# Loading w_down in two row halves per partition instead of row pairs, and the activation product that goes with it

## The chip, the cores and the metric

One Trainium2 chip, one core of it. The time is that of one execution on the device, in microseconds (us), the median of several runs. Engines: PE (TensorE), DVE (VectorE), ACT (ScalarE), POOL (GpSimd), SP (SyncE, which here only issues transfers), and 16 DMA engines that carry out the transfers.

## What is computed

One inference step of a decoder layer for 256 prompt tokens and 8 decode tokens, all float32: a token mixer (retention and gated delta net), then a mixture of experts, and a final norm. The change touches the experts alone. Each token goes to 4 of 32 experts; model and hidden width are both 1024:

```python
def expert_block(args):
    xb, e = args
    hb = (xb @ w_gate_up[e] + b_gate_up[e]).astype(f32)
    glu = jnp.minimum(hb[:, :D_FF], SWIGLU_LIMIT)
    lin = jnp.clip(hb[:, D_FF:], -SWIGLU_LIMIT, SWIGLU_LIMIT)
    act = (glu * jax.nn.sigmoid(SWIGLU_ALPHA * glu) * (lin + 1.0)).astype(xb.dtype)
    return act @ w_down[e] + b_down[e]
```

`w_gate_up` is 32 x 1024 x 2048, `w_down` 32 x 1024 x 1024, 402 MB together, each read once.

## The kernel before, in words

The mixer takes the first third of the time. It loads w_in, the branch weights and w_out in pieces of 2 MB into two slots (`wslot`), with rows of 512 floats (2 KB); the retention states come in rows of 1 KB.

Then come 32 blocks, one for each expert, of 64 token slots each, and after them extra blocks for experts with more tokens, as many as the routing asks for. In a block, PE gathers its tokens by a one-hot product (L1190), transposes them (L1198), multiplies them by gate_up (L1213) into two PSUM banks, and DVE and ACT make the activation: bias (L2300, L2301), clamps, sigmoid (L1648), and as the last product `ac` = `lin` * `sg` (L2313). In `ac` partition 64g+t holds token t and hidden columns 512g to 512g+511. PE transposes `ac` in four tiles of 128 columns (L1222), ACT copies the result to `acT` (L1653), PE multiplies by down (L1237), ACT copies the result to `yb`, and PE adds it to the tokens with the gate weights (L1261, L1268); DVE sums that into X (L2324).

The weights pass through a ring of 16 slots of 1 MiB, 8 KB in each of 128 partitions. SP issues one DMA per slot, in the order of the list `CHUNKS`, written out by hand: for block b four chunks of gate_up, two of down of block b-1, two of gate_up, two of down, two of gate_up; at the end the 8 down chunks of the last two blocks. Before chunk i SP waits until PE has used chunk i-16 (`m_use`). A gate_up chunk is 128 rows of 2048 floats, one row per partition. A down chunk is 256 rows of 1024 floats, two rows per partition. Its matmuls take the two halves of a slot one after the other, each with one column block of `acT`:

```python
for a in range(2):
    for g in range(2):
        t = pe.matmul(home[64 * g:64 * g + 64, :], block_of(acT, 2 * k + a),
                      w[:, D * a + 512 * g:D * a + 512 * g + 512], ...
```

PE works in one fixed order: combine of block b-2, two gate_up chunks of b, transposes of `ac` of b-1, two gate_up chunks, two down chunks of b-1, two gate_up, two down, the gather for b+1, one gate_up, transposes of the tokens, one gate_up. The first four ring chunks are issued during the branch products, eight more (and the first two of down among the next) while w_out is loaded and multiplied; from chunk 16 on each waits for PE.

For an expert known only at run time (an extra block) the same functions `load_chunk` and `activate` are used. The profiled execution has none: L1213 counts 2048 matmuls, 64 for each of 32 blocks.

Of the kernel before, what the change touches and what calls it, by code (L numbers as in the profile page):

```python
# [14 lines left out]
ALU = mybir.AluOpType  # L15
# [6 lines left out]
P = 128  # L22
# [76 lines left out]
def build_layer(nc, d, o):  # L99

    with ExitStack() as ctx:
        base = [-(-nc.sbuf_base // 32) * 32]

        def at(name, offset, shape, dt=F32):
            return nc.alloc_sbuf_tensor_at(name, shape, dt, offset=offset)
# [10 lines left out]
        def sem(name):  # L116
            return ctx.enter_context(nc.semaphore(name))
# [104 lines left out]
        def mnew(name, shape, dt=F32):  # L222
            n = 4
            for x in shape[1:]:
                n *= x
            t = at(name, mb[0], shape, dt)
            mb[0] += -(-n // 32) * 32
            assert mb[0] <= p0 + PREG, mb[0]
            return t
# [17 lines left out]
        xg, glu, lin, xT = [mnew(n, [P, 512]) for n in ("xg", "glu", "lin", "xT")]  # L247
# [13 lines left out]
        sg, ac, acT, yb = [at(n, k0 + 4 * C_NEG + 2048 * i, [P, 512]) for i, n in enumerate(("sg", "ac", "acT", "yb"))]  # L261
        ring = [at(f"ring{k}", (wreg + 65536 + 8192 * k, wreg + 32768 + 8192 * (k - 4), p0 + 8192 * (k - 8),
                                wreg + 8192 * (k - 12))[k // 4], [P, 2 * D]) for k in range(RING)]
# [20 lines left out]
        def half_rows(f):  # L284
            return f.rearrange("p (a n) -> p a n", a=2)

        def half(f, i):

            return f[:, 4 * i:4 * i + 4, :]
# [95 lines left out]
        m_w = [sem(f"m_w{k}") for k in range(RING)]  # L385
# [7 lines left out]
        def after(eng, s, per, b, plus=0):  # L393


            if isinstance(b, int) and b * per + plus <= 0:
                return
            eng.wait_ge(s, b * per + plus)
# [11 lines left out]
        def used(eng, kind, b):  # L410

            if isinstance(b, int):
                if b >= 0:
                    eng.wait_ge(m_use, PLACE[kind, b, KT - 1 if kind == "gate_up" else 3] + 1)
                return
            after(eng, m_use, 12, b, KT if kind == "gate_up" else 12)
# [25 lines left out]
        def _(sp):  # L442
# [28 lines left out]
            for b in range(KT):  # L471
                rows = slice(NBASE * b, NBASE * b + NBASE)
# [5 lines left out]
            for a in range(4):  # L478
                rows, first = slice(32 * a, 32 * a + NBASE), 32 * (a % 2) + NBASE
# [9 lines left out]
            for b in range(KT):  # L489
                rows, first = slice(NBASE * b, NBASE * b + NBASE), NBASE * (b % 4)  # L490
# [56 lines left out]
            def expert(table, e):  # L547
                if isinstance(e, int):
                    return table[0][e]
                return table[0][bass.ds(e, 1)].rearrange("a n m -> (a n) m")  # L550

            def load_chunk(kind, e, k, slot):
                if kind == "gate_up":
                    sp.dma_start(ring[slot][:, :], expert(d["w_gate_up"], e)[P * k:P * k + P, :]).then_inc(m_w[slot], 16)
                else:
                    sp.dma_start(ring[slot][:, :], expert(d["w_down"], e)[2 * P * k:2 * P * k + 2 * P, :].rearrange(  # L556
                        "(p a) n -> p (a n)", a=2)).then_inc(m_w[slot], 16)

            def load_bias(b, e):
                after(sp, m_bb, 1, b, -1)  # L560
# [3 lines left out]
            def load_next(first, last):  # L564
                for i in range(first, last):
                    kind, b, k = CHUNKS[i]
                    if i >= RING:
                        sp.wait_ge(m_use, i - RING + 1)
                    load_chunk(kind, b, k, i % RING)
# [20 lines left out]
            def extra(j, b):  # L590
                e = sp.value_load(xei[0:1, bass.ds(j, 1)], min_val=0, max_val=NE - 1)
                after(sp, m_use, 12, b)
                for k in range(KT):
                    load_chunk("gate_up", e, k, k)
                load_bias(b, e)
                for k in range(4):
                    load_chunk("down", e, k, KT + k)
# [1201 lines left out]
        def _(dve):  # L1799
            link = chain(dve, dve_chain)  # L1800
            v = nc.vector
# [143 lines left out]
            for c in range(2):  # L1945
                for i in range(2):
                    MM.wait(dve, f"QK{i}.{c}")
                    f = half(DT[:, c], i)
# [28 lines left out]
            for c in range(2):  # L1977
# [3 lines left out]
                for q in range(2):  # L1981
                    rows = slice(64 * q, 64 * q + 32)
# [43 lines left out]
            for n, f, first in (("k", k4, 0), ("v", v4, 2 * P)):  # L2026
                MS.wait(dve, "v")
                for j in range(4):
                    rows = slice(32 * j, 32 * j + NB)
# [10 lines left out]
            for j in range(4):  # L2040
                rows = slice(32 * j, 32 * j + NB)
# [117 lines left out]
            for c in range(2):  # L2159
                RA.wait(dve, f"rr{c}")  # L2160
                link(v.tensor_tensor(by_head(oT[c][:, :, :]), by_head(oT[c][:, :, :]), bc(rr[c][:, :, :], 2, 2), ALU.mult))
                f = gT[:, :, P * c:P * c + P]
                RD.did(v.tensor_tensor(f, f, oT[c][:, :, :], ALU.mult), f"g{c}")
            for s in range(4):
                RP.wait(dve, f"out{s}")
                for h in range(RH):
                    f = Ssr[s][:, :, h, :]
# [7 lines left out]
            f = gT[:, :, 2 * P:TOK]  # L2175
# [117 lines left out]
            def activate(b):  # L2293

                used(dve, "gate_up", b)
                if isinstance(b, int) and b == 0:
                    dve.wait_ge(s_bb, 32)
                after(dve, m_bb, 1, b)
                after(dve, m_act, 1, b)
                v.tensor_tensor(glu[:, :], B[0][:, :], bgb[:, 0, :], ALU.add).then_inc(m_b1, 1)  # L2300
                v.tensor_tensor(lin[:, :], B[1][:, :], bgb[:, 1, :], ALU.add).then_inc(m_b2, 1)  # L2301
                after(dve, m_b1, 1, b, 1)
                v.tensor_scalar(glu[:, :], glu[:, :], 7.0, None, ALU.min).then_inc(m_glu, 1)
                after(dve, m_b2, 1, b, 1)
                v.tensor_scalar(lin[:, :], lin[:, :], 7.0, -7.0, ALU.min, ALU.max).then_inc(m_lin, 1)  # L2305
                after(dve, m_lin, 1, b, 1)
                after(dve, m_glu, 1, b, 1)
                v.scalar_tensor_tensor(lin[:, :], lin[:, :], 1.0, glu[:, :], ALU.add, ALU.mult).then_inc(m_lin2, 1)  # L2308
                after(dve, m_lin2, 1, b, 1)
                after(dve, m_sig, 1, b, 1)  # L2310
                after(dve, m_ta, 1, b)
                rows = [f[:, :].rearrange("p (i n a) -> p i n a", n=P, a=2) for f in (lin, sg)]
                v.tensor_tensor(ac[:, :].rearrange("p (i a n) -> p i n a", n=P, a=2), *rows, ALU.mult).then_inc(m_act, 1)  # L2313

            homes = ((B[6], B[7]), (B[2], B[3]))

# [11 lines left out]

            onehot(1, 1)
            activate(0)  # L2330
            dve.wait_ge(s_xaev, 5)
            for b in range(1, NE):
                accumulate(b - 1)
                if b + 1 < NE:
                    onehot(b + 1, b + 1)
                weighted(b - 1, b - 1, b - 1)
                if b == 2:
                    extras()
                activate(b)
# [5 lines left out]
            def extra(j, b):  # L2345
                q = dve.value_load(xqi[0:1, bass.ds(j, 1)], min_val=NE, max_val=NE * NM - 1)
                e = dve.value_load(xei[0:1, bass.ds(j, 1)], min_val=0, max_val=NE - 1)
                onehot(b, q)
                activate(b)
                weighted(b, q, e)  # L2350
                accumulate(b + 1)
                after(dve, m_acc, 3, b, 6)
                dve.sem_inc(m_end)
# [38 lines left out]
```

## Time and profile before

| | us |
|---|---|
| median of 3 runs | 1442.37 |
| lowest, highest | 1439.89, 1442.53 |
| the profiled execution, its own time | 1442.37 |
| its span, first to last instruction | 1440.5 |

| engine | busy us | share of the span |
|---|---|---|
| PE, matmuls | 1387.7 | 96% |
| DVE | 516.9 | 36% |
| ACT | 255.0 | 18% |
| POOL | 108.5 | 8% |

The profile is of one execution. Busy time is that of the instructions themselves; waits stand apart. The shares are means over the span: which resource sets the end in a stretch is read from that stretch. A packet is one contiguous piece that one DMA engine moves. The core read 468.85 MB from memory and wrote 11.26 MB.

### The profile page before, as it was taken

The numbers are of one execution on the slowest core, as the hardware profiler recorded it, in microseconds if no ns is written. First come the engines' busy times: TensorE is split into PE (matmuls) and PEld (weight loads), VectorE is DVE, ScalarE is ACT, GpSimd is POOL, SyncE is SP. The second block draws the span as 40 slices with busy tenths as digits, with TensorE's granted clock in tenths as the row PEclk, the third lists the DMA queues.
The fourth block names the chain that finished last, engine by engine and source line by source line (L and its number), as shares of the span: only waits on it lengthen the run. The fifth ranks groups of instructions, "written<-read, shape, count | busy, mean of one in ns | idle before, by whom it ended". The sixth has DMA issues, their size and how long they took to land.

```text
span 1440.5 us, 18174 instructions
## 1 busy us (share of the span) xinstructions
PE 1387.7 (96%) x7559; PEld 668.5 (46%) x7559; DVE 516.9 (36%) x1097; ACT 255.0 (18%) x465; POOL 108.5 (8%) x107
## 2 busy tenths in 40 slices
PE   8999999999999999999999999999999999999996
PEld 6888985478887433333333332323223332233331
DVE  5655244314112229224323422243222432224323
ACT  3443341122201311011111101111011110111112
POOL 0002110100000001001000100010000100001000
PEclk9999899999999999999999999999999999999999
DMA  7532437544549799999999999999999999999995
GB/s 232 201 126 84 147 103 235 192 162 167 199 138 391 267 408 421 420 421 420 421 421 420 421 420 421 422 421 420 421 420 421 421 421 421 421 421 421 420 421 209
DMA packets 114930, 481.20 MB, mean 334 GB/s; under 512 B 17599, under 2 KB 38511, under 8 KB 65267
## 3 DMA queue, kind: packets, MB, share of 16 engines
q1 hardware_dynamic: 113796, 478.61, 83.4%
q8 instruction: 61, 1.00, 0.3%
q10 hardware_dynamic: 954, 1.07, 0.3%
q0 software_dynamic: 96, 0.33, 0.1%
q14 instruction: 23, 0.19, 0.0%
HBM read 468.85 MB, written 11.26 MB: 333 GB/s over the span
## 4 chain that ended last, share of the span: by engine, by line
PE 60%; DMA 36%; DVE 2%; SPq 1%; issue 1%; ACT 0%; DVEq 0%; ACTq 0%
DMA ring<-in_w_down 36%; PE bank L1213 13%; PE bank L1237 9%; PE bank L688 7%; PE bank L676 6%; PE bank L1085 4%; PE bank L955 4%; PE bank L1190 3%; PE bank L1108 2%; PE bank L1261 2%; DVE Ssg L2073 1%; PE bank L661 1%; SPq L556 1%; PE bank L1198 1%; PE bank L1222 1%; PE bank L948 1%
## 5 line engine op out<-in xcount | busy, mean ns | idle before, releaser
L1213 PE MATMUL bank<-ring,xT 128*64 128x512 f32 x2048 | 477.9, 601 | 6.9 <-DMA ring<-in_w_gate_up 5.5
L1213 PEld LDWEIGHTS bank<-ring,xT 128*64 128x64 f32 x2048 | 134.5, 137 | 277.6 <-issue 247.3
L1237 PE MATMUL bank<-ring,acT 128*64 128x512 f32 x1024 | 236.3, 596 | 21.5 <-DMA ring<-in_w_down 20.8
L2300 DVE TENSOR_TENSOR glu<-bank,bgb 128x512 f32<-128x512 f32 x32 | 22.1, 691 | 598.9 <-PE bank L1213 598.9
L1237 PEld LDWEIGHTS bank<-ring,acT 128*64 128x64 f32 x1024 | 69.8, 137 | 178.9 <-issue 123.1
L688 PE MATMUL bank<-HT,wslot 128*128 128x264 f32 x512 | 119.3, 388 | 0.0
L1787 POOL PARTITION_BROADCAST bgb<-bgu x31 | 40.8, 1316 | 998.4 <-DVE lin L2301 781.4
L688 PEld LDWEIGHTS bank<-HT,wslot 128*128 128x128 f32 x512 | 95.3, 190 | 19.6 <-issue 4.6
L1663 ACT COPY yb<-bank 128x512 f32<-128x512 f32 x32 | 18.7, 586 | 438.0 <-PE bank L1237 438.0
L1190 PE MATMUL bank<-hrow,O 128*64 128x512 f32 (+1 forms) x384 | 94.0, 607 | 0.3 <-DVE O L2231 0.3
L676 PE MATMUL bank<-HT,wslot 128*128 128x264 f32 x384 | 89.6, 394 | 0.8 <-DVE HT L1834 0.8
L2324 DVE TENSOR_TENSOR X<-X,bank 128x512 f32<-128x512 f32 x132 | 81.5, 679 | 15.3 <-PE bank L1261 15.3
L676 PEld LDWEIGHTS bank<-HT,wslot 128*128 128x128 f32 x384 | 74.0, 194 | 15.4 <-issue 2.3
L1261 PE MATMUL bank<-yb,CT 64*128 64x512 f32 x256 | 63.6, 615 | 0.7 <-issue 0.7
L955 PE MATMUL bank<-wslot,HT 128*128 128x512 f32 x128 | 56.0, 596 | 0.6 <-DVE Ssg L2073 0.6
L1190 PEld LDWEIGHTS bank<-hrow,O 128*64 128x64 f32 (+1 forms) x384 | 24.8, 136 | 63.5 <-issue 63.5
L2308 DVE SCALAR_TENSOR_TENSOR lin<-lin,glu 128x512 f32<-128x512 f32 x32 | 48.9, 1529 | 1.1
L2305 DVE TENSOR_SCALAR lin<-lin 128x512 f32<-128x512 f32 x32 | 45.4, 1419 | 0.0
L1653 ACT COPY acT<-bank 128x512 f32<-128x512 f32 x32 | 18.8, 587 | 140.9 <-PE bank L1222 133.6
L1261 PEld LDWEIGHTS bank<-yb,CT 64*128 64x128 f32 x256 | 22.1, 186 | 41.8 <-issue 41.8
L1791 POOL PARTITION_BROADCAST bgb<-bgu x31 | 40.3, 1300 | 6.2 <-POOL bgb L1787 6.2
L955 PEld LDWEIGHTS bank<-wslot,HT 128*128 128x128 f32 x128 | 24.0, 190 | 30.4 <-issue 29.4
(414 smaller groups left out, 1149.0 us busy)
## 6 DMA issues: line engine op xcount, KB each, us to landing
ring<-in_w_gate_up SPq DMA_DIRECT2D x256, 1024.0 KB, 26.6
ring<-in_w_down SPq DMA_DIRECT2D x128, 1024.0 KB, 26.6
wslot<-in_w_in SPq DMA_DIRECT2D x17, 2048.0 KB, 8.0
out<-Ssg SPq DMA_DIRECT2D x8, 512.0 KB, 5.4
Ssr<-in_state_ret SPq DMA_DIRECT2D x4, 1024.0 KB, 10.4
out<-Ssr SPq DMA_DIRECT2D x4, 1024.0 KB, 8.2
wslot<-in_w_branch_b SPq DMA_DIRECT2D x2, 2048.0 KB, 7.9
wslot<-in_w_branch_a SPq DMA_DIRECT2D x2, 2048.0 KB, 7.9
```

Source lines behind the costliest of these rows:

```text
L676: ins = pe.matmul(B[t % 2][:, 0:TOK], wslot[u][:, k, P * m:P * m + P], HT[:, k, :], start=(k == 0), stop=(k == KT - 1))
L688: t = pe.matmul(B[n % 2][:, 0:TOK], wslot[u][:, k, P * m:P * m + P], HT[:, k, :], start=(k == 0), stop=(k == KT - 1))
L955: t = pe.matmul(banks[c][:, :], lhsT[:, k, P * c:P * c + P], w[:, k, :], start=(k == 0), stop=(k == KT - 1))
L1085: t = pe.matmul(B[m % 2][:, 0:TOK], wslot[r % 2][:, k, P * (m % 4):P * (m % 4) + P], (zT if m < KT else gT)[:, k, :], start=(k == 0), stop ...
L1190: t = pe.matmul(B[3][64 * g:64 * g + 64, :], O[0:r, c, :], hrow[0:r, c, 512 * g:512 * g + 512], start=(c == 0), stop=(c == 2))
L1213: t = pe.matmul(B[part][64 * g:64 * g + 64, :], block_of(xT, k), w[:, D * part + 512 * g:D * part + 512 * g + 512], start=(k == 0), stop=( ...
L1237: t = pe.matmul(home[64 * g:64 * g + 64, :], block_of(acT, 2 * k + a), w[:, D * a + 512 * g:D * a + 512 * g + 512], start=(k == 0 and a == ...
L1261: t = pe.matmul(homes[c][g][:, :], CT[64 * g:64 * g + 64, P * c:P * c + P], yb[64 * g:64 * g + 64, :], start=True, stop=True)
L1787: g.partition_broadcast(bgb[:, :, :].rearrange("p t n -> p (t n)"), bgu[:, 1, :, :].rearrange("o t n -> o (t n)")).then_inc(m_bh, 1)
L2305: v.tensor_scalar(lin[:, :], lin[:, :], 7.0, -7.0, ALU.min, ALU.max).then_inc(m_lin, 1)
L2308: v.scalar_tensor_tensor(lin[:, :], lin[:, :], 1.0, glu[:, :], ALU.add, ALU.mult).then_inc(m_lin2, 1)
L2324: t = v.tensor_tensor(f, f, homes[c][g][:, :], ALU.add)
```

## The change

`load_chunk`: in a down chunk, partition p takes rows p and 128+p of the chunk's 256 rows, in place of rows 2p and 2p+1. `activate`: the last product writes `ac` in its natural column order, in place of an order in which even and odd columns of each 256 are set apart for the transposes. Both say which row of `w_down` meets which column of the activation, and they fit each other before and after.

```diff
                 else:
-                    sp.dma_start(ring[slot][:, :], expert(d["w_down"], e)[2 * P * k:2 * P * k + 2 * P, :].rearrange(
-                        "(p a) n -> p (a n)", a=2)).then_inc(m_w[slot], 16)
+                    sp.dma_start(half_rows(ring[slot][:, :]), expert(d["w_down"], e)[2 * P * k:2 * P * k + 2 * P, :].rearrange(
+                        "(a p) n -> p a n", p=P)).then_inc(m_w[slot], 16)
...
-                rows = [f[:, :].rearrange("p (i n a) -> p i n a", n=P, a=2) for f in (lin, sg)]
-                v.tensor_tensor(ac[:, :].rearrange("p (i a n) -> p i n a", n=P, a=2), *rows, ALU.mult).then_inc(m_act, 1)
+                v.tensor_tensor(ac[:, :], lin[:, :], sg[:, :], ALU.mult).then_inc(m_act, 1)
```

`half_rows`, which stands in the kernel before too (L284), views a slot as two halves: `f.rearrange("p (a n) -> p a n", a=2)`.

## Rows read from the trace of the kernel before

**Rows 1.** The page: slices of 36 us, tenths busy; below, all DMA packets.

```profile
PE   8999999999999999999999999999999999999996
...
DMA  7532437544549799999999999999999999999995
GB/s 232 201 126 84 147 103 235 192 162 167 199 138 391 267 408 421 420 421 420 421 421 420 421 420 421 422 421 420 421 420 421 421 421 421 421 421 421 420 421 209
DMA packets 114930, 481.20 MB, mean 334 GB/s; under 512 B 17599, under 2 KB 38511, under 8 KB 65267
```

**Rows 2.** Stretches (us): busy us of each engine, granted clock, DMA share, GB/s.

```profile
core 0: us, PE busy (x) PEld busy (x) DVE busy (x) ACT busy (x) POOL busy (x), PEclk, DMA share, GB/s
...
520.00:830.00 310.00, 310.00 (x1499) 103.53 (x1497) 123.16 (x224) 36.87 (x66) 31.63 (x24) 1.00 1.01 421
830.00:1400.00 570.00, 544.53 (x2575) 172.90 (x2573) 182.17 (x320) 63.71 (x114) 49.45 (x38) 1.00 1.01 421
```

**Rows 3.** The chain that ended last: start us, us, what.

```profile
569.85 3.58 PE bank L1213 x16
...
597.80 3.58 PE bank L1213 x16
...
839.26 27.54 DMA ring<-in_w_down
...
957.51 1.96 PE bank L1237 x8
...
987.34 1.96 PE bank L1237 x8
...
1381.34 28.95 DMA ring<-in_w_down
```

**Rows 4.** DMA, 480 to 520 us, 40 slices of 1 us.

```profile
GB/s 434 426 393 410 434 401 107 25 0 0 0 0 8 0 0 0 106 303 442 369 254 418 352 344 393 360 410 434 426 426 344 344 344 279 418 442 426 418 385 369
```

**Rows 5.** DMA, 600 to 700 us: packets, then queue, packets, MB, share of 16 engines.

```profile
DMA packets 5797, 42.08 MB, mean 421 GB/s; under 512 B 652, under 2 KB 652, under 8 KB 668
...
q1 hardware_dynamic: 5768, 41.98, 101.0%
```

**Rows 6.** DMA, 100 to 104 us, a stretch of the w_in loads.

```profile
DMA packets 781, 1.60 MB, mean 400 GB/s; under 512 B 0, under 2 KB 0, under 8 KB 781
...
q1 hardware_dynamic: 781, 1.60, 104.1%
```

**Rows 7.** DMA, 275 to 277 us, packets of 1 KB and of 2 KB.

```profile
DMA packets 502, 0.77 MB, mean 383 GB/s; under 512 B 16, under 2 KB 240, under 8 KB 502
```

**Rows 8.** SP's queue in order of time: start us, us, issue.

```profile
458.45 1.20 SPq L556 DMA_DIRECT2D ring<-in_w_down  x2
```

**Rows 9.** SP's issues by tile: duration ns min/median/max, first and last start us.

```profile
L556 SPq DMA_DIRECT2D ring<-in_w_down x128: 327/2131/5307, 458.4 to 1396.0; - x128
...
L453 SPq DMA_DIRECT2D wslot<-in_w_in x17: 368/373/1988, 11.8 to 349.0; - x17
```

**Rows 10.** The tail in order of time: start us, us, what, [idle before].

```profile
1407.92 1.08 DVE L2313 TENSOR_TENSOR ac<-lin,sg 128x512 f32<-128x512 f32 x1
...
1412.81 0.20 PEld L1237 LDWEIGHTS bank<-ring,acT 128*64 128x64 f32 x4 [0.19 <-DMA ring<-in_w_down]
...
1414.85 0.58 ACT L1653 COPY acT<-bank 128x512 f32<-128x512 f32 x1 [7.36 <-PE bank L1237]
```

**Rows 11.** Groups by line, 520 to 1441 us: busy us, mean ns, idle before.

```profile
L1222 PE MATMUL bank<-K,ac 128*128 128x128 f32 x124 | 20.3, 286 | 0.0
...
L2262 DVE TENSOR_TENSOR xcmp<-xpre,K 1x512 f32<-1x512 f32 x4 | 2.7, 678 | 0.1
```

**Rows 12.** The tile ac: duration ns min/median/max, and who waited for it.

```profile
L2313 DVE TENSOR_TENSOR ac<-lin,sg x32: 1077/1082/1926, 515.1 to 1407.9; 128x512 f32<-128x512 f32 x32
...
  PEld bank L1222: 24.3, 30
```

**Rows 13.** A weight load of PE in order of time, and its wait.

```profile
903.29 0.42 PEld L1198 LDWEIGHTS bank<-K,xg 128*128 128x128 f32 x4 [0.81 <-issue]
```

## The prediction

> **What bounds the kernel now.** I read the page from its slices first [rows 1]. From the fifteenth of 40 slices on, which is nearly the whole mixture-of-experts part, PE and DMA both show 9, and the bytes per second stand at 420 to 422 GB/s in slice after slice. Two full rows cannot both be the limit, so the order in which they give way has to be found. The stretches [rows 2] tell it: from 520 to 830 us PE is busy 310.00 of 310.00 us, from 830 to 1400 us only 544.53 of 570.00, and the DMA share (1.01) and rate (421 GB/s) are the same in both. The chain that ended last [rows 3] says it in pieces: at 569.85 and 597.80 us it runs on PE, one expert block every 27.95 us, and from 839.26 us on it is one long piece after another of "DMA ring<-in_w_down", with the eight matmuls of a down chunk starting at 957.51 and 987.34 us, one block every 29.83 us. A block brings 12 chunks of 1 MiB, 12.58 MB, and 12.58 MB at 421 GB/s are 29.9 us. So the transfers are the slower of the two from the start; PE lives on the 16 ring slots filled ahead, loses about 1.9 us of this lead per block, and has used it up by 839 us. What sets the end is the landing of the down chunks; the last one in the chain lands at 1410.29 us, followed by 30 us of PE, ACT and DVE work. The granted clock is 1.00 throughout [rows 2], the 2.4 GHz level, so the clock is no term here.
>
> Where the stream becomes continuous is read from the DMA view of 480 to 520 us [rows 4]: it falls to 0 GB/s from 488 to 495 us, because all 16 slots are full and PE has not begun, and is at full load from about 498 us, when the first slots come free. What was transferred ahead of this gap has its cost absorbed in it; what comes behind it counts in full.
>
> **The change, part by part.**
>
> *The load of a down chunk.* Before, partition p takes rows 2p and 2p+1 of the chunk, which lie behind each other in memory: one piece of 8 KB. After, it takes rows p and 128+p: two pieces of 4 KB. The bytes, the number of DMAs, the slot, the semaphore and the place in the order stay. 128 DMAs change; each has 128 pieces now, 8 per DMA engine, and 256 after, 16 per engine. So the cost is 8 more packets per engine and chunk, and its price is what a packet costs besides its bytes.
>
> No stretch of this trace has 4 KB packets alone, so I bound that price with packets on both sides. In the ring's stream, 600 to 700 us [rows 5], 5797 packets went, 668 of them under 8 KB: 5129 of 8 KB in 16 engines x 100 us = 1600 us, 312.0 ns each. In a stretch of the w_in loads, 100 to 104 us [rows 6], 781 packets of 2 KB went in 64 us: 81.9 ns each. If a packet costs a fixed part and a part per byte, 2 KB are (312.0 - 81.9)/3 = 76.7 ns, and the fixed part is 5.2 ns: 8 x 5.2 = 42 ns per chunk. That is the low end. By the packets' own times (101.0% and 104.1% of the engines in the same rows, so 315.1 and 85.3 ns) the same sum gives 8.7 ns, 70 ns per chunk. And from 275 to 277 us [rows 7] 224 packets of 1 KB go with 262 of 2 KB; taking 81.9 ns for each of the latter, 10.5 of the 32 us are left, 47.1 ns per 1 KB packet; against the 8 KB packets the fixed part is then 47.1 - (312.0 - 47.1)/7 = 9.3 ns, 74 ns per chunk. That is the high end. Below nothing I don't go: in all three stretches the smaller packet costs more per byte. The 4 KB packet lies between the sizes measured, no row is clearly nearer, and I take the mean of the three, 62 ns per chunk, on 2.49 us: a stream of down chunks at 411 GB/s where gate_up stays at 421.
>
> The Trainium skill has a figure for this shape: in "DMA: Bandwidth & Descriptors", section "iDMA fabric — 4 AXI ports for 8 engines, asymmetric across TPBs", a load stream of 1 MiB per DMA with 4 KiB rows ran at 408.7 GB/s on a core alone. By that page a down chunk would take 2.57 us, 75 ns more than at the 421 GB/s of [rows 5], and the sum below would be 9.1 us; the same page's "Specifications" calls 512 B enough for line rate, by which the sum would be nothing (1442.4 us, a rival below).
>
> How many chunks count: of the 128 down chunks the first two are issued at 458.45 us [rows 8], ahead of the gap. The last chunk whose landing is in the chain is the third of block 30; the fourth lands right behind it (the weight load waits 0.19 us for it at 1412.81 [rows 10]), and the four of block 31 land while PE is occupied with the work before them. 128 - 2 - 4 = 122 chunks, 122 x 0.062 = 7.6 us. The chunks just behind the gap, where the queue is still short, could make this some 3 chunks less, 0.2 us.
>
> *SP's issue.* The same 128 instructions. SP stands 2.13 us (median) in the issue of a chunk [rows 9], and still waits for PE's use of slots after it. If that were the time to write the pieces, doubling would hurt (a rival, below). But a 2 MB load of w_in, with 1024 pieces, is issued in 0.37 us [rows 9]; the 2.13 us are a queue that is full. I cost it at nothing. Behind SP's issues there are only further ring loads, so nobody else waits.
>
> *The activation's last product, L2313.* The interleaved write becomes a plain one. Before it takes 1082 ns (median) [rows 12]; the nearest plain one on 512 elements of SBUF, L2262, takes 678 ns [rows 11]. So DVE gets 0.40 us back 32 times, 12.9 us of its time, and `ac` is ready 0.40 us earlier. What hides this: PE is in a pair of gate_up chunks when DVE makes `ac`, the transposes' weight load does wait 0.81 us each time for it (24.3 us in 30 [rows 12]), but it waits the same 0.81 us as "issue" ahead of other groups [rows 13], and the transposes' matmuls show no idle PE before them at all, 0.0 us [rows 11]. And even where PE gained, a faster PE only runs into the ring's landings sooner. In the tail, `ac` of the last block is done at 1409.00 us and the copy behind its transposes starts only at 1414.85, when PE has used the previous `acT` [rows 10]. I cost it at nothing; with the cover gone it would be 0.40 x 31 = 12.4 us of gain. The transposes, the copy to `acT`, and the down matmuls keep their shapes: the order of the 1024 rows changes alike in the weights and in `ac`.
>
> The sum: 7.6 + 0 + 0 us on the profiled execution's own 1442.37 us (span 1440.5, 1.9 around it), which is also the median of the three runs: 1450.0 us, 0.5% slower. By the two ends: 122 x 42 ns = 5.1 us gives 1447.5, 122 x 74 ns = 9.0 us gives 1451.4.
>
> **The rivals.**
>
> *The extra packets cost nothing that can be measured* (within 0.2%, 2.9 us, about what a measurement of this kernel can tell). The mechanism here: a DMA engine overlaps the fixed part of a packet with the bytes of the one before, and 4 KB is long enough. The share above 100% [rows 5, 6] speaks for some overlap. Against it: the overlap is in the 81.9 ns already, and 5.2 ns are still left. Price 0 to 2.9 us, 1442.4 to 1445.3. 12%. The Trainium skill's 512 B rule, quoted above, would have it so.
>
> *A fixed part per packet that is larger than in my rows*, because rows 512 KB apart are read in turn. The 1 KB packets reach 9.3 ns with 1 KB rows from many places, so I see nothing for more; doubling it, 148 ns per chunk, gives 18 us, 1460. 6%.
>
> *SP's issue becomes the bound.* If 2.13 us per chunk grew with the pieces, a block's issues would be 8 x 2.13 + 4 x 4.26 = 34.1 us against 29.83: 4.3 us in each of 30 blocks, 1570 us. It decides once an average issue passes 2.49 us. Against it stand the 0.37 us above. 2%.
>
> *Faster: the earlier `ac` reaches the end.* Place: PE's transposes of `ac`. If PE's time there were really set by DVE, and PE rather than the transfers set the end, 31 x 0.40 = 12.4 us would go, 1430 us. It decides only from the point where a block's transfers take less than PE's 27.95 us, and they take 29.83 now. 4%.
>
> **How the numbers follow.** Forecast, slower by 5.1 to 9.0 us and a little beyond on either side (3 to 11 us): 76%. With the rivals: faster by over 0.2% 4%, within 0.2% 12%, slower by over 0.2% 84% (76 + 6 + 2). The predicted time is the likeliest one's, 1450.0. The range reaches from 1444.0 (it takes in the upper half of the case without a cost) to 1453.5 (the high end, and the runs' spread of some 2 us), and leaves out the two large losses, the gain and half of the free case, about 18%.
>
> **What the profile after would show.** The packets' count rises by 128 x 128 = 16,384, from 114,930 to about 131,300, all of it "under 8 KB". The rate in the full slices falls from 421 to some 417 or 418 GB/s with the DMA share still at 1.01, and the distance of down chunks in the chain from 29.83 to about 30.07 us. The chain turns from PE to DMA earlier than 839 us, since the lead goes at 2.1 us per block. L2313 shows about 0.68 us, the transposes still 0.0 us of idle PE before them. SP's issues stay at some 2 us. The prediction is wrong if the rate stays at 421 (the free case), if SP's issue of a down chunk is near 4 us, or if DMA share falls under 1.

## The result: 0.6% slower, and the profile after

| | us |
|---|---|
| median before, 4 runs | 1441.13 |
| median after, 4 runs (1449.85 to 1450.70) | 1450.01 |
| ratio, 95% interval | 1.0064 (1.0047 to 1.0083) |
| span of the profiled execution after | 1448.3 |

The kernel became slower by 8.9 us (the interval says 7 to 12). 1450.0 us was forecast, with a cost of 7.6 us on 1442.4 us. That the two times meet is partly luck: the median of before is 1.2 us lower with the fourth run in, and the cost 1.3 us higher.

The page after, the lines that answer to [rows 1]:

```profile
PE   8999999999999999999999999999999999999996
...
DMA  7532537645549799999999999999999999999995
GB/s 237 194 126 84 155 95 235 207 149 181 176 165 395 291 396 416 417 416 417 417 417 416 416 417 418 417 416 416 417 417 417 417 417 416 419 417 416 416 416 203
DMA packets 131314, 481.20 MB, mean 332 GB/s; under 512 B 17599, under 2 KB 38511, under 8 KB 98035
```

The bytes are the same 481.20 MB; the packets are 16,384 more, all of them under 8 KB, and the full slices are at 416 to 419 GB/s where they were at 420 to 422.

The stretches, as in [rows 2] (busy us of each engine, granted clock, DMA share, GB/s):

```profile
520.00:830.00 310.00, 310.00 (x1499) 103.54 (x1497) 120.09 (x223) 36.94 (x66) 31.00 (x24) 1.00 1.02 416
830.00:1400.00 570.00, 536.66 (x2533) 168.44 (x2531) 172.70 (x312) 63.20 (x113) 49.47 (x38) 1.00 1.02 417
```

From 830 to 1400 us PE is idle for 33.3 us where it was 25.5: the loss shows as PE waiting longer for the ring, at a DMA share that is full as before.

The chain that ended last, as in [rows 3]:

```profile
815.78 22.64 DMA ring<-in_w_down
...
962.00 2.72 PE bank L1190 x12
...
990.42 1.94 PE bank L1237 x8
...
1020.86 1.94 PE bank L1237 x8
...
1387.37 2.72 PE bank L1190 x12
```

It turns from PE to the transfers at 816 us, 23 us earlier than before: PE's lead is used up sooner. Such a piece of the chain begins with the issue of a transfer, and PE first waits at its end. The first waits for the ring (idle time in brackets), before and after:

```profile
864.36 1.94 PE L1237 MATMUL bank<-ring,acT 128*64 128x512 f32 x8 [0.36 <-DMA ring<-in_w_down]
```

```profile
833.36 1.94 PE L1213 MATMUL bank<-ring,xT 128*64 128x512 f32 x8 [0.44 <-DMA ring<-in_w_gate_up]
```

So the lead ends at 864.0 us before and at 832.9 us after, about one block earlier. From 962.00 to 1387.37 us are 14 blocks, 30.38 us each.

The tail in order of time (compare [rows 10] and the third down chunk of block 30, whose landing was at 1410.29 us in [rows 3]):

```profile
1415.33 0.69 DVE L2312 TENSOR_TENSOR ac<-lin,sg 128x512 f32<-128x512 f32 x1
...
1417.95 1.94 PE L1237 MATMUL bank<-ring,acT 128*64 128x512 f32 x8 [0.63 <-DMA ring<-in_w_down]
...
1422.55 0.59 ACT L1653 COPY acT<-bank 128x512 f32<-128x512 f32 x1 [7.64 <-PE bank L1237]
```

PE starts on that chunk at 1417.95 us, 7.6 us later, and what follows takes as long as it did; the two spans differ by 7.8 us. The ring's stretch has grown by more than that, since PE's first gate_up product comes 1.6 us earlier in this execution: from it to the third chunk of block 30 it was 1410.33 - 491.9 = 918.4 us and is 1417.95 - 490.3 = 927.6 us, 9.2 us longer. The line of that product in the kernel before, and in the one after (duration in ns min/median/max, first and last start):

```profile
L1213 PE MATMUL bank<-ring,xT x2048: 592/592/1114, 491.9 to 1404.6; 128*64 128x512 f32 x187
```

```profile
L1213 PE MATMUL bank<-ring,xT x2048: 592/592/1061, 490.3 to 1412.0; 128*64 128x512 f32 x187
```

The product in front of the transposes, L2312, takes 0.69 us in place of 1.08, and `acT` still waits for PE, as before.

### The profile page after: what moved, and what is told of

Same layout as the page of the kernel before. It is cut to its first block, busy times and chain, and to the rows that moved or that the text cites. A ratio compares the mean times of both kernels' runs of the same rounds, so it can differ in the third digit from the quotient of the medians.

```text
span 1448.3 us, 18174 instructions
## 1 busy us (share of the span) xinstructions
PE 1387.2 (96%) x7559; PEld 666.8 (46%) x7559; DVE 507.5 (35%) x1097; ACT 255.3 (18%) x465; POOL 108.1 (7%) x107
## 2 busy tenths in 40 slices
DMA packets 131314, 481.20 MB, mean 332 GB/s; under 512 B 17599, under 2 KB 38511, under 8 KB 98035
## 4 chain that ended last, share of the span: by engine, by line
PE 64%; DMA 33%; DVE 2%; issue 0%; ACT 0%; DVEq 0%; ACTq 0%
DMA ring<-in_w_down 33%; PE bank L1213 14%; PE bank L1237 9%; PE bank L688 7%; PE bank L676 6%; PE bank L1190 6%; PE bank L1085 4%; PE bank L955 4%; PE bank L1108 2%; PE bank L1261 2%; DVE Ssg L2073 1%; PE bank L661 1%; PE bank L1198 1%; PE bank L948 1%; PE bank L1247 0%
## 5 line engine op out<-in xcount | busy, mean ns | idle before, releaser
L1663 ACT COPY yb<-bank 128x512 f32<-128x512 f32 x32 | 18.8, 587 | 446.8 <-PE bank L1237 446.8
L1653 ACT COPY acT<-bank 128x512 f32<-128x512 f32 x32 | 18.8, 589 | 141.5 <-PE bank L1222 133.9
```

## The experiments

Times are medians; each ratio is to the kernel before on the same chip, as recorded, and can differ by 0.1% from that of the two medians. The kernel before had 1441.71 us (17 runs) beside the first four experiments, 1443.42 us (9 runs) beside the next four and 1440.96 us (7 runs) beside the last two.

| kernel | median us | ratio, 95% interval | against before, us |
|---|---|---|---|
| load only | 1448.90 | 1.0044 (1.0031 to 1.0057) | +7.2 |
| activation only | 1442.16 | 0.9997 (0.9984 to 1.0010) | +0.5 |
| two pieces 12 KB apart | 1449.86 | 1.0046 (1.0029 to 1.0062) | +8.2 |
| down in 2 KB pieces | 1467.02 | 1.0176 (1.0161 to 1.0190) | +25.3 |
| 16 KB pieces | 1431.17 | 0.9919 (0.9902 to 0.9935) | -12.3 |
| half of each down chunk left out | 1401.45 | 0.9717 (0.9699 to 0.9736) | -42.0 |
| the same, plain activation product | 1401.70 | 0.9706 (0.9685 to 0.9727) | -41.7 |
| the same, half chunks in 2 KB pieces | 1402.49 | 0.9720 (0.9702 to 0.9738) | -40.9 |
| all of the ring in 4 KB pieces | 1467.23 | 1.0175 (1.0153 to 1.0198) | +26.3 |
| all of the ring in 2 KB pieces | 1521.29 | 1.0547 (1.0520 to 1.0575) | +80.3 |

### Each half of the change alone

The load alone is the first hunk of the change's diff on the kernel before.

> The new load with the old activation product: the rows of w_down meet other columns of the activation than they should, so the values differ from the reference's, while every instruction keeps its size. Theory of the packets (each extra packet has a fixed price on a DMA engine, and the transfers set the end): all of the change's 8.9 us, so 7 to 10 us over the kernel before, rate near 417 GB/s, 131,300 packets. Rival, the activation has a part in it: less than 5 or more than 12 us here.

The activation alone is the second.

> The old load with the new activation product (values differ from the reference's in the same way). Theory of the packets: within 1.5 us of the kernel before, L2312 at 0.69 us instead of 1.08, rate 421 GB/s, chain unchanged. Rival, the 0.39 us per block reach the end: up to 12 us faster. Rival, the change's 8.9 us are a net of a dearer load and a gain of DVE: a gain here of several us, with the load alone costing the same more.

The load alone costs 7.2 us and has the rate and the packets of after; the activation alone moves nothing outside the noise, with L2312 at 692 ns (median). The whole of the loss belongs to the load, and DVE's gain of 0.39 us per block reaches nobody. The two add up to 7.7 us against the change's 8.9, within what the intervals allow.

A time of the whole kernel also holds what varies ahead of the ring: PE's first gate_up product starts between 490 and 495 us in the traces of these kernels. The ring's own stretch, from that start to the landing of the third chunk of block 30, leaves it out. The lines for the load alone, then for the activation alone:

```profile
L1213 PE MATMUL bank<-ring,xT x2048: 592/592/1112, 492.6 to 1413.8; 128*64 128x512 f32 x187
...
1392.34 27.34 DMA ring<-in_w_down
```

```profile
L1213 PE MATMUL bank<-ring,xT x2048: 592/592/1116, 494.8 to 1407.5; 128*64 128x512 f32 x187
...
1384.41 28.77 DMA ring<-in_w_down
```

The landings are at 1419.68 and 1413.18 us, so the stretch is 927.1 us with the load alone and 918.4 us with the activation alone, against 918.4 us in the kernel before (landing at 1410.29 us) and 927.6 us after. The load costs the ring 8.7 to 9.2 us, and the activation nothing.

### Is it the distance between the two pieces, or their number

```diff
-                    sp.dma_start(half_rows(ring[slot][:, :]), expert(d["w_down"], e)[2 * P * k:2 * P * k + 2 * P, :].rearrange(
-                        "(a p) n -> p a n", p=P)).then_inc(m_w[slot], 16)
+                    if isinstance(e, int):
+                        first = (D * e + 2 * P * k - (2 if (e, k) == (NE - 1, 3) else 0)) * D
+                        rows = bass.AP(d["w_down"].tensor, first, [[2 * D, P], [3 * D, 2], [1, D]])
...
+                    sp.dma_start(half_rows(ring[slot][:, :]), rows).then_inc(m_w[slot], 16)
```

Experts known only at run time keep the load of after; none occurs.

> The kernel after, but partition p takes rows 2p and 2p+3 of the table instead of p and 128+p: again two pieces of 4 KB, 12 KB apart instead of 512 KB (rows of w_down are mixed up, so the values differ). Theory of the packets: the same as after, 7 to 10 us over before. Rival, the distance in memory is what costs: within 2 us of before. In between, say 4 us, both have a part.

It cost 8.2 us with the pieces 12 KB apart, much as with 512 KB, and its ring's stretch is 927.6 us (from 490.2 to a landing at 1417.83 us), the same as after. So the number of pieces costs, not how far apart they lie; the rival with rows 512 KB apart falls.

### Three times the dose

```diff
-                    sp.dma_start(half_rows(ring[slot][:, :]), expert(d["w_down"], e)[2 * P * k:2 * P * k + 2 * P, :].rearrange(
-                        "(a p) n -> p a n", p=P)).then_inc(m_w[slot], 16)
+                    rows = expert(d["w_down"], e)[2 * P * k:2 * P * k + 2 * P, :]
+                    sp.dma_start(ring[slot][:, :].rearrange("p (g a n) -> p g a n", g=2, a=2),
+                                 rows.rearrange("(a p) (g n) -> p g a n", p=P, g=2)).then_inc(m_w[slot], 16)
...
-                                          w[:, D * a + 512 * g:D * a + 512 * g + 512],
+                                          w[:, D * g + 512 * a:D * g + 512 * a + 512],
```

> The kernel after with each row of a down chunk cut into two pieces of 2 KB (the two halves of a row lie apart in the slot): 32 packets per engine and chunk instead of 16, so 24 more than before. Theory of a fixed price per packet: the 8.9 us of 8 extra packets times 3, 24 to 29 us over before, a rate near 410 GB/s. If the price is the 5.2 ns that the 2 KB stream gave, 122 x 24 x 5.2 ns = 15 us. If pieces of 2 KB and more cost alike and only the first split counts, 9 us.

25.3 us for 24 extra packets per engine and chunk, against 8.9 for 8: in proportion, within the intervals (23.2 to 27.4 us here). Per packet that is 25.3 us / (122 x 24) = 8.6 ns.

### The other direction: pieces of 16 KB

```diff
+        pair = [at(f"ring{k}", (wreg + 65536 + 8192 * k, wreg + 32768 + 8192 * (k - 4), p0 + 8192 * (k - 8),
+                                wreg + 8192 * (k - 12))[k // 4], [P, 4 * D]) for k in range(0, RING, 2)]
+        ring = [pair[k // 2][:, 2 * D * (k % 2):2 * D * (k % 2) + 2 * D] for k in range(RING)]
...
                 if kind == "gate_up":
...
+                    rows = expert(d["w_gate_up"], e)[2 * P * r:2 * P * r + 2 * P, :].rearrange("(p a) n -> p (a n)", a=2)
                 else:
...
+                    rows = expert(d["w_down"], e)[4 * P * r:4 * P * r + 4 * P, :].rearrange("(p a) n -> p (a n)", a=4)
+                if both:
+                    sp.dma_start(pair[slot // 2][:, :], rows).then_inc(m_w[slot], 16)
...
+                    hrow[0:r, c, 512 * g:512 * g + 512].rearrange("p (i a n) -> p i n a", i=2, a=2),
+                    hbanks[n][0:r, :].rearrange("p (i n a) -> p i n a", i=2, a=2), ACT.Copy,
...
+                rows = [f[:, :].rearrange("p (n m) -> p n m", m=4) for f in (lin, sg)]
+                v.tensor_tensor(ac[:, :].rearrange("p (m n) -> p n m", m=4), *rows, ALU.mult).then_inc(m_act, 1)
```

`r` is `k // 2`. A DMA for a pair waits until both slots are used, and PE waits for it at both chunks.

> The other direction, with the whole computation in it: one DMA fills two neighbouring slots with 2 MiB, 16 KB per partition (two rows of w_gate_up, or four rows of w_down), for all chunks but the first 16 and the last 8; the token rows are put in the matching column order once, by ACT, and ac by the last product. That is 4 packets fewer per engine and chunk. By the price per packet that the runs so far showed (25.3 us / (122 x 24) = 8.6 ns), 360 chunks x 4 x 8.6 ns = 12.4 us less than before, 1427 to 1432 us, rate 427 GB/s. Rival, the coarser grain costs more than it gives (a DMA waits for two free slots, PE for two landed ones): at or above before. Rival, packets over 8 KB are not cheaper per byte: no change in the rate.

12.3 us faster than before. The kernel after is 8.9 us slower than before, so this version beats it by some 21 us. The DMA view of it from 600 to 700 us, a part of its chain, and SP's issues of the pairs (ns min/median/max):

```profile
DMA packets 2950, 42.67 MB, mean 427 GB/s; under 512 B 331, under 2 KB 331, under 8 KB 347
```

```profile
858.47 33.20 DMA ring<-in_w_down
891.71 3.65 PE bank L1251 x16
...
950.78 3.65 PE bank L1251 x16
...
1010.08 3.65 PE bank L1251 x16
```

```profile
L566 SPq DMA_DIRECT2D ring<-in_w_gate_up x121: 327/328/328, 499.7 to 1357.9; - x121
```

Half the packets at a higher rate, 427 GB/s, and two blocks in 59.1 to 59.3 us. The coarser grain costs nothing that the total shows: 12.4 us were expected from the packets alone. The transfers still set the end, since 29.6 us per block is above PE's 27.95.

### The transfers made lighter, so that PE is the bound

```diff
+                elif light:
+                    sp.dma_start(ring[slot][:, 0:D], expert(d["w_down"], e)[2 * P * k:2 * P * k + 2 * P, :].rearrange(
+                        "(p a) n -> p (a n)", a=2)[:, 0:D]).then_inc(m_w[slot], 16)
```

> The kernel before with half of each down chunk left unloaded from the 17th chunk on (only row 2p into the first half of the slot; PE multiplies what stands there, so the values differ). A block's transfers then take 8 x 2.49 + 4 x 1.27 = 25.0 us, less than PE's 27.95. If the transfers set the end before, PE runs at 27.95 us per block to the end and 19 blocks x 1.9 us go: 1405 to 1417 us. If something else held the pace, less than 10 us go.

The second has the change's activation product besides; the third has this load:

```diff
+                    sp.dma_start(half_rows(ring[slot][:, 0:D]), expert(d["w_down"], e)[2 * P * k:2 * P * k + 2 * P, 0:512].rearrange(
+                        "(a p) n -> p a n", p=P)).then_inc(m_w[slot], 16)
```

> The same lightened kernel with the plain activation product: PE sets the pace throughout, so this is where a gain of DVE would show. Prediction's reading (PE never waits for ac): within 1 us of the lightened kernel. Rival (the 0.39 us per block reach PE): up to 12 us less.

> The same lightened kernel, its half chunks of 512 KB in pieces of 2 KB instead of 4 KB: again 8 more packets per engine and down chunk, the change's own number, but with PE as the bound. If a packet's price is paid on the DMA engines alone it is hidden here: within 1 us of the lightened kernel. Rival (the packets also cost SP, or the latency of landings): 5 to 9 us more.

42.0 us went, and 1401.45 us lies outside the 1405 to 1417 us that were expected. The stretches of the first, and its transposes of `ac`:

```profile
520.00:830.00 310.00, 310.00 (x1501) 103.49 (x1499) 123.08 (x223) 36.87 (x66) 31.63 (x24) 1.00 0.96 376
830.00:1350.00 520.00, 520.00 (x2511) 173.60 (x2507) 174.61 (x310) 62.47 (x112) 46.92 (x37) 1.00 0.96 376
```

```profile
L1225 PE MATMUL bank<-K,ac 128*128 128x128 f32 x124 | 20.3, 286 | 0.0
```

PE is busy throughout and the DMA share has fallen under 1. So it was the transfers that set the end before. With PE as the bound, the plain activation product changes nothing (1401.70 against 1401.45 us), which settles the rival of the earlier `ac`: no idle PE stood ahead of the transposes in either regime. And 8 more packets per engine and down chunk, the change's own number, cost 1.0 us there, within the intervals of nothing: in this kernel the price of a packet is paid only where the DMA engines are the bound.

The expectation was too small because it took a block at 29.83 us. Over 12 blocks of the kernel before the chain gives (1227.41 - 866.84)/12 = 30.05 us, so 2.1 us go per block, and the expectation's 19 blocks give 40 us:

```profile
866.84 1.96 PE bank L1237 x8
...
1227.41 1.96 PE bank L1237 x8
```

PE's idle time shows only a part of this. The engines' line of the lightened kernel:

```profile
PE 1373.6 (98%) x7559; PEld 673.4 (48%) x7559; DVE 516.6 (37%) x1097; ACT 255.0 (18%) x465; POOL 108.5 (8%) x107
```

Of the 40.9 us between the spans of the two profiled executions (1440.5 and 1399.6) 26.8 are idle time of PE, and 14.1 are busy time (1387.7 against 1373.6), for the same 7559 matmuls: presumably the profile, which models where matmuls end, books a part of each wait as busy time; no run shows that by itself.

### The price by itself, in streams of one size

```diff
+                if isinstance(e, int):
+                    wide = 2 if kind == "gate_up" else 1
+                    first = D * D * wide * e + P * 2 * D * k
+                    rows = bass.AP(d["w_" + kind].tensor, first, [[1024, P], [1024 * P, 2], [1, 1024]])
+                    sp.dma_start(ring[slot][:, :].rearrange("p (a n) -> p a n", n=1024), rows).then_inc(m_w[slot], 16)
```

> The kernel before with every ring chunk, gate_up too, cut into 256 pieces of 4 KB, pieces p and 128+p to partition p (the weights land in other places than they should, so the values differ; sizes and order stay). A stream of one size, which measures the price itself: 8 more packets on 364 chunks behind the gap (122 down, 242 gate_up). At the 8.6 ns of the mixed streams 25 us over before, 1467 us, 409 GB/s; at the 5.2 ns that the prediction's low end took from the 2 KB stream of w_in, 15 us, 1457 us, 414 GB/s.

For 2 KB the 1024 is 512 and the 2 is 4.

> The same in 512 pieces of 2 KB: 24 more packets per engine on 364 chunks (values differ as above). If the price is the same 8.6 ns whatever the neighbours, 75 us over before, 1518 us, 387 GB/s. If a stream of 2 KB packets alone runs as the w_in load did, 81.9 ns each, the ring's stream runs at 400 GB/s and 45 us are added, 1488 us. It tells whether that load was a poor measure of this price or whether the mixing of sizes costs extra.

The DMA views from 600 to 700 us, first the stream in 4 KB pieces, then that in 2 KB pieces:

```profile
DMA packets 10608, 40.90 MB, mean 409 GB/s; under 512 B 629, under 2 KB 629, under 8 KB 10603
```

```profile
DMA packets 19449, 38.67 MB, mean 387 GB/s; under 512 B 597, under 2 KB 597, under 8 KB 19444
```

1600 engine-us over 10603 - 629 = 9974 packets are 160.4 ns for 4 KB, and over 19444 - 597 = 18847 packets 84.9 ns for 2 KB. With 312.0 ns for 8 KB [rows 5] and 1600 us / (2950 - 347) = 614.7 ns for 16 KB, all in the ring's own stream (the few small packets between, completions above all, are left inside these times):

| bytes | ns per packet | 75.7 ns per 2 KB + 9.2 ns |
|---|---|---|
| 2 KB | 84.9 | 84.9 |
| 4 KB | 160.4 | 160.6 |
| 8 KB | 312.0 | 312.0 |
| 16 KB | 614.7 | 614.8 |

One straight line holds all four. Two mixed streams test it, that of after (4 and 8 KB) and that of the kernel with down in 2 KB pieces (2 and 8 KB), from 600 to 700 us:

```profile
DMA packets 7323, 41.68 MB, mean 417 GB/s; under 512 B 644, under 2 KB 644, under 8 KB 3826
```

```profile
DMA packets 10243, 40.95 MB, mean 409 GB/s; under 512 B 629, under 2 KB 629, under 8 KB 6789
```

3182 packets at 160.4 ns and 3497 at 312.0 ns make 1601 us, 6160 at 84.9 ns and 3454 at 312.0 ns make 1601 us, and 1600 engine-us are there. So a packet of the ring's stream costs 9.2 ns beside its bytes, whatever its neighbours. The figure that the Trainium skill gives in "DMA: Bandwidth & Descriptors", section "iDMA fabric — 4 AXI ports for 8 engines, asymmetric across TPBs", 408.7 GB/s for 1 MiB loads with 4 KiB rows, is met by the 409 GB/s here.

## Why the prediction was right, point by point

**The bound.** Right. The transfers set the end: with lighter transfers PE alone gives 1401 us, and the load's packets cost only where the transfers are the bound. One reading was off: PE's lead isn't used up by 839 us, where the chain's transfer is issued, but at 864.0 us, where PE first waits for one. The cost doesn't hang on it, since it is counted on the transfers.

**The number of packets.** Right: 16,384 more, as counted, none merged.

**The price of a packet.** The mechanism was right, the term `122 x 0.062 = 7.6 us` was sized too small. The price is 9.2 ns, 74 ns per chunk, where 62 ns were taken, and 122 x 74 ns = 9.0 us, which was the high end, against 8.9 us measured and 8.7 to 9.2 us in the ring's stretches. The times of whole kernels don't tell 9.0 from 7.6 us: the change's interval is 7 to 12 us, that of the load alone 4.5 to 8.2, that of the pieces 12 KB apart 4 to 9. The streams and stretches of the traces tell it. What pulled the mean down was the 5.2 ns from the w_in load, at 81.9 ns per packet of 2 KB [rows 6], where the ring's stream needs 84.9 ns for the same size. A difference of 3 ns in 82 becomes 4 ns of the 9, since the fixed part is a small rest of two large numbers. Why w_in's packets run 3 ns quicker isn't settled; the experiment in 2 KB pieces shows that it is not the mixing of sizes. The bound from 1 KB packets was good: just behind [rows 7] the kernel before has them alone, the retention states' load from 277 to 279 us, at 32 us / 679 = 47.1 ns, and the line gives 37.85 + 9.2 = 47.1 ns.

```profile
DMA packets 679, 0.70 MB, mean 348 GB/s; under 512 B 0, under 2 KB 679, under 8 KB 679
```

The sum by the Trainium skill's 408.7 GB/s, 9.1 us, was the best single estimate; that figure is for a stream of 1 MiB loads with rows of 4 KiB, the shape of the new chunks.

**The number of chunks.** 122 fits: 25.3 us for 24 packets on 122 chunks is 8.6 ns, and on 364 chunks the all-4-KB ring gives 26.3 us / (364 x 8) = 9.0 ns and the all-2-KB ring 80.3 us / (364 x 24) = 9.2 ns.

**SP's issue.** Right. The median issue of a down chunk is 2130 ns, as before. In the lightened kernel, where the transfers keep up, a half chunk of 128 pieces is issued in 328 ns (median), and in its version with 2 KB pieces one of 256 pieces in 378 ns:

```profile
L556 SPq DMA_DIRECT2D ring<-in_w_down x126: 327/328/328, 493.5 to 1348.4; - x126
```

```profile
L556 SPq DMA_DIRECT2D ring<-in_w_down x126: 367/378/379, 495.0 to 1349.7; - x126
```

So the doubled pieces cost SP 50 ns, and the rest of the 2.13 us is waiting that goes when the transfers get lighter, as a full queue would have it.

**The activation product.** Right, costed at nothing: 0.69 us instead of 1.08, and no effect alone, nor with PE as the bound.

**What the profile would show.** The rate was forecast at 417 or 418 GB/s and is 416 to 419; the chain turned to the transfers earlier, at 816 us. The distance of down chunks was forecast 0.24 us longer and is 0.33 us longer (30.38 against 30.05 us, over 14 and 12 blocks; 4 x 74 ns would be 0.30); the 29.83 us that the prediction read off a single pair of blocks was not a good mean.

**The rivals.** The free case (12%) fell with the rate: even from 8 to 16 KB the rate still rises, from 421 to 427 GB/s. The distance of 512 KB, SP's issue and the earlier `ac` were each tried or read off and fell.

## What to carry to other kernels

Where a stream of transfers sets the end, count its packets as well as its bytes: in this kernel's ring each contiguous piece costs its DMA engine a fixed 9 ns, 3% of an 8 KB piece, 11% of a 2 KB one. Choosing which rows share a partition decides the size of the piece, and a permutation of the other operand that makes the pieces longer is worth a slower instruction on an engine off the path: here 0.4 us of DVE per block stand against 0.3 us per block of the transfers, and only the latter count. To find such a price, read it from a stream of the same shape, or from sizes far apart; the rest of a difference between two sizes magnifies 3 ns into half the answer.

## What was not expected of the hardware

- The line through 2, 4, 8 and 16 KB is straight to within 0.2 ns from 600 to 700 us (the four stretches of 100 us behind it give 612.6 to 614.7 ns for 16 KB), and 16 KB per partition still gains over 8 KB: 427 against 421 GB/s.
- Not every stream lies on it. The w_in loads take 81.9 ns per 2 KB, and the kernel before stores its retention states in 1 KB packets, alone from 358 to 362 us, at 64 us / 1510 = 42.4 ns each, where the load of the same states takes 47.1. Both stay open.

```profile
DMA packets 1528, 1.55 MB, mean 387 GB/s; under 512 B 18, under 2 KB 1528, under 8 KB 1528
```

- The time from issue to landing of a ring chunk (median) falls as the packets shrink, from 26.6 us with 8 KB to 18.8 with 4 KB and 14.5 with 2 KB (the whole ring in that size), without any loss of rate beyond the packets' price. That is about 85, 117 and 171 packets per engine, so the queue ahead of the engines is neither a fixed number of bytes nor of packets. In the 16 KB kernel it is 32.0 us for a pair of down and 33.1 us for one of gate_up, and SP is never held up in the issue of a pair. What limits the queue stays open.
